# Eight pieces of x, each ahead of its weights, transposes two units ahead, blank matmuls and squares at a new place in an encoder kernel

## What is computed

```python
def rms_norm(x, g):
    xf = x.astype(jnp.float32)
    y = xf * lax.rsqrt(jnp.mean(xf * xf, axis=-1, keepdims=True) + EPS)
    return (y * g.astype(jnp.float32)).astype(x.dtype)

def mixer_ab(xn, w_in, w_out, a_qn, a_kn, a_rpb, b_qn, b_kn):
    s = xn.shape[1]
    h = xn @ w_in
    ...

def reference(x, attn_norm, ffn_norm, ...):
    for layer in range(DEPTH):
        j = layer // 2
        xn = rms_norm(x, attn_norm[layer])
        if layer % 2 == 0:
            x = x + mixer_ab(xn, ab_w_in[j], ...)
        else:
            x = x + mixer_cd(xn, cd_w_in[j], ...)
        x = x + swiglu(rms_norm(x, ffn_norm[layer]), w_gate[layer], w_up[layer], w_down[layer])
    return x
```

## Time and profile before

| | |
|---|---|
| runs of the kernel before | 2131.4, 2131.78, 2133.42 us |
| time of the profiled execution | 2131.87 us |
| its span, first to last instruction | 2130.1 us |
| PE busy | 2117.8 us, 99% |
| DVE, ACT, POOL busy | 1367.0, 1001.1, 79.5 us |
| HBM read | 406.07 MB |
| start of the first weight matmul | 11.30 us |
| start of unit 8, the first of the second column tile | 36.53 us |

### The profile page before, as it was taken

The page is one execution under the profiler, slowest core; times in us unless marked ns, Lnnn a source line. Parts: engine busy times, 40 slices in busy tenths (PEclk is TensorE's granted clock), DMA queues, the critical chain, the costliest instruction groups (busy, mean ns, idle before and its releaser), DMA issues.

```text
span 2130.1 us, 27641 instructions
## 1 busy us (share of the span) xinstructions
PE 2117.8 (99%) x9424; PEld 1748.4 (82%) x9424; DVE 1367.0 (64%) x1810; ACT 1001.1 (47%) x1253; POOL 79.5 (4%) x85
## 2 busy tenths in 40 slices
PE   8999999999999999999999999999999999999999
PEld 7888888888888888888887788888888888888887
DVE  6666667676667766666675766586676667755443
ACT  6555545444444444444455566554444444444443
POOL 0110011000000000000011000010000000000000
PEclk9999999999999999999999999999999999999999
DMA  8766666666666665555667664666666666656664
GB/s 272 233 197 188 198 208 199 187 188 200 198 192 186 188 205 186 184 190 196 211 216 239 186 190 149 201 196 196 187 188 205 190 196 181 193 187 205 210 204 141
DMA packets 221874, 418.78 MB, mean 197 GB/s; under 512 B 14832, under 2 KB 25328, under 8 KB 221808
## 3 DMA queue, kind: packets, MB, share of 16 engines
q1 hardware_dynamic: 219360, 413.71, 62.4%
q10 hardware_dynamic: 2448, 4.21, 0.6%
HBM read 406.07 MB, written 11.80 MB: 196 GB/s over the span
## 4 chain that ended last, share of the span: by engine, by line
PE 94%; DMA 2%; DVE 1%; issue 1%; ACT 1%; POOL 1%; SPq 0%; ACTq 0%
PE psum L490 30%; PE psum L493 30%; PE psum L491 30%; PE psum L556 2%; PE psum L536 1%; DMA w_raw<-in_cd_w_in 1%; PE psum L510 1%; DMA block_dram<-turn_sb 1%; POOL head_rstd L1307 0%; ACT w_hi L628 0%; SPq L443 0%; DVE turn_sb L1036 0%; PE psum L554 0%; DVE w_lo L894 0%; DMA x_res<-in_x 0%
## 5 line engine op out<-in xcount | busy, mean ns | idle before, releaser
L894 DVE TENSOR_TENSOR w_lo<-w_raw,w_hi 128x1024 fp32r<-128x1024 f32 x760 | 907.5, 1200 | 638.7 <-ACT w_hi L628 633.4
L628 ACT ACTIVATE w_hi<-w_raw 128x1024 fp32r<-128x1024 f32 x760 | 786.9, 1041 | 955.1 <-PE psum L493 918.8
L490 PE MATMUL psum<-w_hi,xt_hi 128*128 128x512 f32 x2016 | 794.3, 394 | 1.5 <-DVE w_lo L894 1.2
L493 PE MATMUL psum<-w_hi,xt_lo 128*128 128x512 f32 x2016 | 785.5, 390 | 0.0
L491 PE MATMUL psum<-w_lo,xt_hi 128*128 128x512 f32 x2016 | 785.2, 389 | 0.0
L490 PEld LDWEIGHTS psum<-w_hi,xt_hi 128*128 128x128 f32 x2016 | 378.8, 188 | 81.9 <-issue 1.9
L493 PEld LDWEIGHTS psum<-w_hi,xt_lo 128*128 128x128 f32 x2016 | 378.7, 188 | 79.9
L491 PEld LDWEIGHTS psum<-w_lo,xt_hi 128*128 128x128 f32 x2016 | 379.0, 188 | 77.7
L490 PE MATMUL psum<-w_hi,ht_hi 128*128 128x512 f32 x960 | 377.6, 393 | 0.3 <-DVE stage L927 0.3
L493 PE MATMUL psum<-w_hi,ht_lo 128*128 128x512 f32 x960 | 373.8, 389 | 0.0
L491 PE MATMUL psum<-w_lo,ht_hi 128*128 128x512 f32 x960 | 373.6, 389 | 0.0
(11 more groups left out here) (100 smaller groups left out, 638.2 us busy)
## 6 DMA issues: line engine op xcount, KB each, us to landing
w_raw<-in_w_gate SPq DMA_DIRECT2D x176, 512.0 KB, 3.7
w_raw<-in_w_up SPq DMA_DIRECT2D x176, 512.0 KB, 3.8
w_raw<-in_w_down SPq DMA_DIRECT2D x160, 512.0 KB, 4.2
w_raw<-in_cd_w_in SPq DMA_DIRECT2D x80, 512.0 KB, 4.2
w_raw<-in_ab_w_in SPq DMA_DIRECT2D x72, 512.0 KB, 4.2
w_raw<-in_ab_w_out SPq DMA_DIRECT2D x32, 512.0 KB, 4.1
w_raw<-in_cd_w_out SPq DMA_DIRECT2D x32, 512.0 KB, 3.7
block_dram<-turn_sb SPq DMA_DIRECT2D x18, 512.0 KB, 2.9
```

Source lines behind the costliest of these rows:

```text
L490: nc.tensor.matmul(acc, hi[:, chunk, ts], w_hi[:, slot, c, :], start=first and c == 0, stop=False)
L493: mm = nc.tensor.matmul(acc, lo[:, chunk, ts], w_hi[:, slot, c, :], start=False, stop=end)
L628: nc.scalar.activation(w_hi[:, slot, 0:n, :], w_raw[:, slot, 0:n, :], ACT.Copy).then_inc(hi_ready, 1)
L894: nc.vector.tensor_tensor(w_lo[:, slot, 0:n, :], w_raw[:, slot, 0:n, :], w_hi[:, slot, 0:n, :].bitcast(F32), ALU.subtract).then_inc(lo_rea ...
```

## The change

x comes in eight pieces of 256 columns, one fill each, and piece u is issued ahead of the weight unit u. The identity's load goes from SP's queue to ACT's. DVE clears 512 columns of `stage[3]`, and PE then does six 128x512 matmuls in bfloat16 on those zeros into the bank OBANK, before it waits for the identity. Fills 0 and 1 are transposed before unit 0, and fill k+2 right after unit k. ACT and DVE take fill 0 ahead of the split of unit 0 and fill 1 behind it; from k = 2 on they take fill k behind the split of unit k. The squares of the four 512-column parts of x are done on ACT behind the splits of units 7, 8, 9 and 10, the sum on DVE behind its split of unit 10.

```diff
@@ -51,6 +51,7 @@
 
 DOWN_UNITS = [(k, 2) for k in range(0, 20, 2)] + [(k, 1) for k in range(20, 24)] + [(k, 2) for k in range(24, HC, 2)]
 DU = len(DOWN_UNITS)
+WARM = 6
 assert DU % RING == 0 and KU % RING == 0 and sum(n for _, n in DOWN_UNITS) == HC
 
 
@@ -270,8 +271,9 @@
         cd_rot_sb = sb("cd_rot_sb", [P, 4, 2, 32])
 
 
-        x_loaded = [sem(f"x_loaded{j}") for j in range(XT)]
+        x_loaded = [sem(f"x_loaded{h}") for h in range(KU)]
         ident_loaded = sem("ident_loaded")
+        warm_ready = sem("warm_ready")
         const_loaded = sem("const_loaded")
         const2_loaded = sem("const2_loaded")
         cd_const_loaded = sem("cd_const_loaded")
@@ -406,9 +408,10 @@
                 rows = src[c0 * P:(c0 + n) * P, cols].rearrange("(c p) n -> p c n", p=P)
                 sp.dma_start(w_raw[:, slot, 0:n, :], rows).then_inc(w_loaded[slot], 16)
 
-            def load_input(j):
+            def load_input(h):
+                cols = slice(h * UC * P, (h + 1) * UC * P)
                 xv = x.rearrange("(t p) n -> p t n", p=P)
-                sp.dma_start(x_res[:, :, j * N:(j + 1) * N], xv[:, :, j * N:(j + 1) * N]).then_inc(x_loaded[j], 16)
+                sp.dma_start(x_res[:, :, cols], xv[:, :, cols]).then_inc(x_loaded[h], 16)
 
 
             def move_blocks(layer, v):
@@ -448,14 +451,13 @@
                          (gain_x[:, 2:4, :], ffn_gain, const2_loaded), (cd_rot_sb[:], cd_gain_rot, const2_loaded),
                          (bias_sb[:, 0], a_bias[0], bias_loaded[0]), (bias_sb[:, 1], a_bias[1], bias_loaded[1])]
 
-            sp.dma_start(ident_sb[:], ident).then_inc(ident_loaded, 16)
             load_input(0)
             for layer in range(2):
                 m = mixers[layer]
                 for p, (col, _, _) in enumerate(m.tiles):
                     for k in range(KU):
                         u = ph["in", layer]["u"] + KU * p + k
-                        if 1 <= u < XT:
+                        if 1 <= u < KU:
                             load_input(u)
                         move_blocks(layer, KU * p + k)
                         load(u, k % RING, w_in[layer], UC * k, UC, slice(col * N, col * N + N), first=u < RING)
@@ -557,23 +559,24 @@
                                                       start=kind in "ab", stop=True)
                         mm.then_inc(l_full, 1)
 
-            def input_transposes(j):
-
-                pe.wait_ge(x_loaded[j], 16)
-                for half in range(2):
-                    wait_t_free(2 * j + half)
-                    transposes(lambda c, tok: x_res[:, tok, (4 * j + 2 * half + c) * P:(4 * j + 2 * half + c + 1) * P],
-                               half)
-
+            def input_transposes(h):
+
+                pe.wait_ge(x_loaded[h], 16)
+                wait_t_free(h)
+                transposes(lambda c, tok: x_res[:, tok, (2 * h + c) * P:(2 * h + c + 1) * P], h % 2)
+
+            pe.wait_ge(warm_ready, 1)
+            blank = stage[3][:, 0, :].bitcast(BF16)
+            for _ in range(WARM):
+                nc.tensor.matmul(psum[:, OBANK, :], blank[:, 0:P], blank[:, 0:N], start=True, stop=True)
             pe.wait_ge(ident_loaded, 16)
             input_transposes(0)
+            input_transposes(1)
             for layer in range(2):
                 m, pi, po, pu, pd = mixers[layer], *(ph[s, layer] for s in ("in", "out", "up", "down"))
                 for p in range(len(m.tiles)):
                     for k in range(KU):
                         t = KU * p + k
-                        if layer == 0 and p == 0 and k % 2 == 0 and k // 2 + 1 < XT:
-                            input_transposes(k // 2 + 1)
                         if p == 0:
 
                             if layer == 0:
@@ -581,6 +584,8 @@
                             else:
                                 pe.wait_ge(tile_split, split_count(0, "down", k))
                         unit(pi["u"] + t, k % RING, xt_hi, xt_lo, (2 * k, 2 * k + 1), 0, pi["a"] + p, k == 0, k == KU - 1)
+                        if layer == 0 and p == 0 and k + 2 < KU:
+                            input_transposes(k + 2)
                         attention(layer, t)
 
                 for i, (n, k) in enumerate(OUT_UNITS):
@@ -791,17 +796,18 @@
                             act.dma_start(bias_sb[:, h % 2], a_bias[h + 2]).then_inc(bias_loaded[h % 2], 16)
 
 
+            act.dma_start(ident_sb[:], ident).then_inc(ident_loaded, 16)
             act.dma_start(gain_x[:, 0:2, :], attn_gain).then_inc(const_loaded, 16)
             act.wait_ge(const_loaded, CONST)
 
             nc.scalar.activation(table_warm[:], gain_x[:, 0, 0:1], ACT.Exp, scale=0.0)
 
-            def input_hi(j):
-                for half in range(2):
-                    fill_to_xt(2 * j + half + 1, half, 4 * j + 2 * half, 0, 4 * j + 2 * half)
+            def input_hi(h):
+                fill_to_xt(h + 1, h % 2, 2 * h, 0, 2 * h)
 
             def input_ssq(j):
-                act.wait_ge(x_loaded[j], 16)
+                for h in (2 * j, 2 * j + 1):
+                    act.wait_ge(x_loaded[h], 16)
                 if j:
                     act.wait_ge(ssq_done, j)
                 for tok in range(TOK):
@@ -817,11 +823,15 @@
                         u = pi["u"] + KU * p + k
                         if k == LEAD and p:
                             evacuate(layer, p - 1)
-                        if layer == 0 and p == 0 and k % 2 == 0:
-                            input_hi(k // 2)
+                        if u == 0:
+                            input_hi(0)
                         split(u, k % RING, ring_full=u >= RING)
-                        if layer == 0 and p == 0 and k % 2 == 1:
-                            input_ssq(k // 2)
+                        if u == 0:
+                            input_hi(1)
+                        if layer == 0 and p == 0 and k >= 2:
+                            input_hi(k)
+                        if layer == 0 and 7 <= u < 7 + XT:
+                            input_ssq(u - 7)
                         attention(layer, KU * p + k - LEAD)
                         if layer == 1 and p == 0 and k == LEAD + 3:
                             residual_hi(0, "down", XT - 1)
@@ -887,6 +897,7 @@
         @block.vector
         def _(dve):
             step = Steps(dve, dve_step)
+            nc.vector.memset(stage[3][:, 0, :], 0.0).then_inc(warm_ready, 1)
 
             def split(u, slot, n=UC):
 
@@ -1179,10 +1190,9 @@
                                                           rdenom[:, s, tok:tok + 1], None, ALU.mult)
                         ins.then_inc(probs_ready, 1)
 
-            def input_lo(j):
-
-                for half in range(2):
-                    fill_to_xt(2 * j + half + 1, half, 4 * j + 2 * half, 0, 4 * j + 2 * half)
+            def input_lo(h):
+
+                fill_to_xt(h + 1, h % 2, 2 * h, 0, 2 * h)
 
             for layer in range(2):
                 m, pi, po, pu, pd = mixers[layer], *(ph[s, layer] for s in ("in", "out", "up", "down"))
@@ -1191,10 +1201,14 @@
                     for k in range(KU):
                         if layer == 1 and p == 0 and k == LEAD - 1:
                             residual_add(0, "down", XT - 1)
-                        if layer == 0 and p == 0 and k % 2 == 0:
-                            input_lo(k // 2)
+                        if layer == 0 and p == 0 and k == 0:
+                            input_lo(0)
                         split(pi["u"] + KU * p + k, k % RING)
-                        if layer == 0 and p == 0 and k == KU - 1:
+                        if layer == 0 and p == 0 and k == 0:
+                            input_lo(1)
+                        if layer == 0 and p == 0 and k >= 2:
+                            input_lo(k)
+                        if layer == 0 and p == 1 and k == 2:
                             mean_square(0)
                         attention(layer, KU * p + k - LEAD)
                         if layer == 1 and p == 0 and LEAD - 1 <= k < LEAD + 3:
```

## The result

The changed kernel takes 2138.2 us (median of 8 runs, 2137.4 to 2139.6), the kernel before 2131.97 us beside it (8 runs, 2129.4 to 2133.5). The ratio is 1.0029, 95% interval 1.002 to 1.0038: 6 us slower. The profiled execution took 2138.20 us with a span of 2136.4, 6.3 us more than the profiled execution of before. The forecast was 2137.8.

What follows compares the result with a forecast made beforehand. The prediction took PE, busy 99% of the span, as the bound. To the profiled 2131.87 us it added 4.3 for a later unit 8 and 1.6 for the low clock behind PE's pause: 2137.8 us, range 2134.4 to 2140.3.

Steps and rivals of the forecast that it cites:

- Bound and slack: Whole run: PE is one unbroken line from 11.30; unit 8 had 0.24 us to spare, `rstd` was 4.0 us early.
- Start of unit 0: First weight matmul at 9.1 instead of 11.30, by x issued 0.47 us earlier and 1.0 us for fewer bytes; bounds 8.1 to 10.0.
- the weights: Ahead of unit 0: w0 lands at 6.2, which allows a start at 8.7, not later than 9.1.
- The identity and the gain: Loads on ACT's queue at the beginning: identity lands at 2.9, under x's landing at 4.6; cost nothing.
- The blanks: Six matmuls ahead of the first transposes: done by 4.5 at the latest, cost nothing, gain taken as nothing.
- Rival C: Blanks bring the clock up, unit 0 at 0.23 a matmul: 2136.2 with slow restart, 2134.6 without; chance 0.15.
- Unit 0 at the low clock: First unit of weight matmuls: lasts 4.36 us as before, matmuls 0.43 us apart.
- Fills: Fills 2 to 7 between units: 0.40 us each, 0.8 us paid back, unit 5 ends at 29.2.
- The list on ACT: Behind unit 5: fill 7, squares, splits, sum, factor and evacuation take 11.66 us against PE's 5.9, so PE stands 5.8 us.
- Clock behind the hole: From unit 8 on: after standing 5.8 us PE restarts at the low clock, costing 1.6 us.
- rival B: Unit 8: PE stands ahead of it but restarts at full clock, 2136.2 us; chance 0.17.
- Rival D: Unit 8: PE does not stand ahead of it, it starts at 35.1, time 2130.4 us, not slower; chance 0.10.

Runs made afterwards that it cites:

- blanks throughout: Changed kernel with squares in ACT's idle time, plus five blank matmuls between fills 0 and 1 and one behind fill 1: 2130.44 us, ratio 0.9989.

## Why the prediction was right

- **Bound and slack.** As told: PE is one line, and the slack ahead of unit 8 was what the squares used up. PE's waits before were read from two rows of four: 1.1 us for low parts of x ahead of unit 0 and 0.3 us for a residual (L927) stand in the view too, and change nothing.
- **Start of unit 0: 9.1 foretold, 9.06 measured**, but by two errors that cancel. x landed at 0.73 + 3.4 = 4.13 and not 4.6; w0 landed at 1.25 + 5.3 = 6.55 and not 6.2, and it, not x, set the split. The step that mattered was the one given as a check, the weights. In four later profiles unit 0 began right behind fill 1, whose piece of x landed late (7.66 to 7.87); the forecast does not name that path.
- **The identity and the gain: "cost nothing" was right by 0.05 us.** With the identity ahead of it the gain took 4.1 us to land where it had taken 1.9, and ACT's first high part came at 5.43, right behind the table's warming at 5.33, where 1.13 us behind the transposes would have been 5.38.
- **The blanks.** Clearing took 0.48 us, the six ran from 1.45 to 4.2, nothing gained in the first profile: all as told. Rival C's mechanism is real, as the runs with blanks throughout show; what did not pay is six blanks with a pause of 1.9 to 2.5 us behind them. The ground I gave against it, that transposes with a pause had not brought the clock up, says nothing of matmuls.
- **Unit 0 at the low clock: mis-sized.** 4.36 us foretold, 4.98 measured (ten slow matmuls, in the kernel before seven). Over the profiles here without further blanks ahead of unit 0 the number runs from three to twelve, so no forecast from one profile could have it closer than by luck.
- **Fills: mis-sized a little.** Unit 5 ended at 30.13, not 29.2. Apart from unit 0, five fills and units took 16.1 us and not 15.75: each fill is 0.35, but the matmul behind it 0.09 longer, and matmuls were 0.230 apart rather than 0.228.
- **The list on ACT: 11.66 foretold, 11.49 measured; hole 5.8 against 5.55.** Each term came out within some 0.1 us: 0.63, 0.73, four pairs of squares of 1.22, three splits of 0.95, factor 1.24, evacuation 0.84. This is the term that decided, and it was a sum of rows.
- **Clock behind the hole: 1.6 foretold, 1.4 measured**, and 1.3 by the blanks put into it. That it falls was shown in all three profiles with a wait of 5.4 us, so rival B is out. That the size fits is in part luck: it was 1.4 us here, 1.6 without blanks and 2.5 in the changed kernel's second profile. The Trainium skill (TensorE: Matmul & The Clock Gate, Why this matters for your kernels) warns of pauses of a few microseconds; the trace agrees for 5.4 us, and the pause of 2.2 us in the kernel before with late squares left the clock up.
- **Rival D** is out by the wait of 5.4 us and by both runs that move the squares.

Sum of the measured steps: -2.24 at the start, +1.78 from there to where unit 8 could begin (27.01 against 25.23), +5.55 hole, +1.40 clock: 6.5 us. The forecast had -2.2, +0.8, +5.8 and +1.6: unit 8 came 0.7 us later than foretold, by unit 0 and the fills, and 0.2 us less for the clock and 0.2 us elsewhere took half of that back. The range's lower end, 2134.4, doesn't follow from its own terms: B with the early start gives 2135.2, B and C together with it 2133.6. The measured time lies far from either.

## What to carry to other kernels

When a step is moved back to make room at the start, look up who reads its result and count the moved list, in program order on its engine, against the work that its reader has left: here 9.1 us of a list on ACT, 11.5 with the sum, the factor and the evacuation, against 5.9 us of PE. ACT's idle time farther ahead of the reader held the same squares for all but 0.5 us. Blank matmuls paid here where they ran on nearly to the real work; six of them with a pause of 2 us behind did not.

## What the runs showed of the hardware that I had not expected

- **The granted clock of the record is silent at the start.** With matmuls 0.43 us apart it read 1.00 in the first profile, but 0.50 for the same pace in an execution where the clock had come up before and fell again, and behind the hole. At the start the distance of matmuls is the thing to read.
- **Pauses, and what PE did before them.** 2.2 us after 24 us of work: the clock stays. 1.65 us with eleven blanks and four transposes before: it stays. 1.88, 2.44 and 2.47 us with six blanks and four transposes before: it falls 0.8 to 1.3 us after the pause. Inside the hole it fell 4.1 to 5.2 us after PE's last matmul (three profiles). These are one to three profiles each; no run changes only the length of the pause or only the work before it.
- **POOL's two small instructions took 3.0 us instead of 0.9** (1.19 + 1.78 against 0.19 + 0.71) when DVE worked without a break, and 0.9 again when put into DVE's idle time. The first ended 0.05 us after the subtraction that ran when it started (33.29 against 33.24), the second 0.56 us after DVE's product (35.15 against 34.59). In the kernel before DVE began its next subtraction at 31.06, in the middle of POOL's second one, and that still took 0.71. So what DVE was doing when POOL's instruction started goes with the delay. The Trainium skill (GPSIMD Engine Reference, Specifications) says that the SBUF interfaces are shared with VectorE, in contention with instructions that read two SBUF inputs; DVE's subtraction and its product are such instructions, and the trace agrees.
- **16 KB behind 64 KB on the same queue** landed after 3.0 to 4.1 us in the eight profiles with this order (4.1 in the first), instead of 1.9, with x and weights loading beside them. What part the order and what part the traffic has in it was not tried.
